# Turning the value product of a windowed attention: values as weights, probabilities moving, division ahead of the transposes

## Chip, core and metric

The kernel runs on one core of one Trainium2 chip. The metric is the device time of one launch in microseconds; the median of several runs counts. Inputs and outputs are float32.

## What is computed

Two layers of a decoder trunk over 512 positions of width 1024. In each layer three mixers work side by side on one input projection and feed one output projection; a gated feed-forward (width 2816) and a gated embedding term follow. The change touches only the third mixer, a causal attention over a window of 128 with six query heads on two key/value heads, and a learned sink per head:

```python
kb, vb = banded(k), banded(v)          # chunk c and chunk c - 1, 128 keys each
sc = einsum('bcqhgd,bckhd->bchgqk', qb, kb) * HEAD_DIM ** -0.5
sc = where(in_window & ~first_pad, sc, NEG_INF)
probs = softmax(concatenate([sc, sink], -1), -1)[..., :-1]
o = einsum('bchgqk,bckhd->bcqhgd', probs, vb)
...
mix = concatenate([y_a, y_b, y_c], -1) @ w_out[i]
```

The positions are cut into four chunks of 128 (c = 0 to 3). Chunk 0 has no chunk before it.

## The kernel before

All five engines run through one list of events, made by `plan_schedule`; each engine picks from it what is its own, in that order, and the engines wait for each other by semaphores alone. So the list sets the order of every queue. A weight strip is loaded by DMA into `raw`, rounded by ScalarE into `w_hi` (float32r, L880), and its remainder is subtracted by VectorE into `w_lo` (L1113); every large product is three float32r products (`mm3`, L616 to L618). That rounding is an event `conv`, put behind every strip, three strips ahead of its use.

The mixers are spread between the blocks of the input projection by `plan_mixers`. A slot u is one block: strip (u div 4) for the 128 positions m = u mod 4, 12 products of 384 columns (slots 12 to 35) or of 512 (36 to 43), and then what `plan_mixers` has put at u. The strips from slot 12 on are bk (12 to 19), bq (20 to 27), bv (28 to 35), a (36 to 43), bg (44 to 51). In slots 16 to 19 and 24 to 27 VectorE also has `rope_full` for each block (five operations, L1134 to L1146).

A chunk c of the attention starts at slot u = 13, 18, 24, 29 and takes these steps:

- `swa_cur` (u) and `swa_prev` (u + 1): scores of the two halves of the window (L758), each into two PSUM banks, `swa_bank(c, 0)` and `swa_bank(c, 1)` (banks 4 and 5 for even chunks, 6 and 7 for odd ones), three heads in each. ScalarE copies the first half to `prob` (L971). VectorE then overlays the second half by a predicated copy (`later_m`, L1237), so that both halves of the window lie in one tile of 128 x 128 for each head: each query sees exactly 128 keys. VectorE forms the maxima (L1239 to L1242), ScalarE the exponentials and their sums (L979) and that of the sink (L982).
- `swa_PT` (u + 4): TensorE transposes the six tiles (L766); VectorE masks them twice, lower triangle to `ptl` (L1249) and, from chunk 1 on, upper triangle to `ptu` (L1251).
- `swa_o` (u + 6): for each head one product with `ptl` and one with `ptu` as the weights (128 keys x 128 queries), 64 columns of values moving (L775, L778). The output has queries on the partitions. VectorE multiplies it by the reciprocal of the sum into `swa_y` (L1257 to L1260).
- `swa_yT` (u + 9): three transposes (L786) bring it to features on the partitions; ScalarE and VectorE split it into `y_hi` (L869) and `y_lo` (L1162).

A float32 product is two instructions in the trace, a transpose and a float32r product are one. The first retention events follow at slots 34 to 38: `ret_T` (L800), `ret_sc` (L808), `ret_o` (L821 to L830), in banks 4 and 5; `ret_T` of chunk 1 in slot 38 waits for the state that VectorE updates from `ret_o` of chunk 0 in slot 37 (L1295, L1296). `ret_T` of chunk 0 waits for y_lo of attention chunk 2, and scores of chunk c for y_lo of chunk c - 2.

Of the kernel before, what the change touches and what calls it, by code (L numbers as in the profile page):

```python
# [16 lines left out]
F32 = mybir.dt.float32  # L17
# [3 lines left out]
ALU = mybir.AluOpType  # L21
# [55 lines left out]
def plan_mixers():  # L77

    at = {}

    def put(u, *e):
        at.setdefault(u, []).append(e)

    for c in range(TILES):

        put(9 + c, "swa_T", c)
        u = (13, 18, 24, 29)[c]
        for step, name in ((0, "swa_cur"), (1, "swa_prev"), (4, "swa_PT"), (6, "swa_o"), (9, "swa_yT")):
# [193 lines left out]
TABLE_W = _at  # L282


def build_trunk(nc, depth, x_in, p_t, pre_mix, w_in, ln_w, ln_b, ws_t, bs_t, gn_w, sinks, w_out,
                post_mix, pre_ffn, w_ffn_in, w_ffn_out, post_ffn, w_gate, w_ple, ple_norm,
                table, later, out):
# [3 lines left out]
    def place(name, shape, dt, kb):  # L291
        return nc.alloc_sbuf_tensor_at(name, shape, dt, offset=BASE + int(kb * KB))
# [31 lines left out]
    swa_y = [place(f"swa_y{i}", [P, C_HEADS, HD], F32, (110, 48)[i]) for i in range(2)]  # L324
# [67 lines left out]
    def sem(name):  # L392
        sems[name] = nc.alloc_semaphore(name)
        return sems[name]
# [39 lines left out]
    swa_exp = sem("swa_exp")  # L434
    swa_PT = sem("swa_PT")
    swa_PTm = sem("swa_PTm")
    swa_o = sem("swa_o")
    swa_yr = sem("swa_yr")


    ret_T = sem("ret_T")
# [35 lines left out]
    last_use = {layer * NS + SIDX[strip]: i for (layer, strip, _), i in order_mm.items()}  # L477
    order_yT = []
    for layer, e in schedule:
        if e[0] in ("swa_yT", "ret_yT", "gmlp_yT"):  # L480
            order_yT += [(layer, e)] * (2 if e[0] == "gmlp_yT" else 1)

    def y_count(layer, e):
# [72 lines left out]
    with nc.Block() as block:  # L556
# [57 lines left out]
        def _(pe):  # L614
# [48 lines left out]
            def block_of(layer, strip, m):  # L663
                g = layer * NS + SIDX[strip]
                kind, _, i = strip
                pe.wait_ge(lo_ready, 2 * (g + 1))
                if kind == "in":
                    last = mm_in(layer, g, strip, m)
                elif kind == "out":
                    if i == 3:  # L670
                        if m < 2:
                            pe.wait_ge(*evac(layer, GNAMES[-1], 2 * m + 1))
                        if m == 2:
                            pe.wait_ge(y_lo_ready, y_count(layer, ("ret_yT", 3)))

                    need = {2: ("ret_yT", m), 3: ("swa_yT", m), 1: ("ret_yT", m), 0: ("gmlp_yT",)}[i]
                    if m == 3:
                        need = ("gmlp_yT",)
                    pe.wait_ge(y_lo_ready, y_count(layer, need))
                    last = mm_rows(y_hi, y_lo, 2 * i, g, m, i == 3, i == 0)  # L680
                elif kind == "ffn":
                    if m is not None:

                        pe.wait_ge(h_lo_ready, t_count(layer, "ffn", max(2 * m + 1, i)))
                    else:
                        if i >= 4:
                            pe.wait_ge(mid_lo_ready, layer * FCH + i - 3)
                        else:
                            pe.wait_ge(h_lo_ready, t_count(layer, "ffn", 3))
                    last = mm_ffn(layer, g, strip, m)  # L690
                elif kind == "fo":
                    if i == 0:
                        last_in_pair = max(j for j in range(FCH) if j % 4 == m)
                        pe.wait_ge(mid_lo_ready, layer * FCH + last_in_pair + 1)
                    pe.wait_ge(mid_lo_ready, layer * FCH + 2 * i + 2)
                    last = mm_rows(mid_hi, mid_lo, 2 * i, g, m, i == 0, i == FCH // 2 - 1)
                elif kind == "ple":
                    pe.wait_ge(h_lo_ready, t_count(layer, "gate", m))
                    pe.wait_ge(p_lo_ready, layer + 1)
                    last = mm_rows(p_hi, p_lo, 0, g, m, True, True)  # L700
# [25 lines left out]
            for layer, e in schedule:  # L726
# [17 lines left out]
                elif kind in ("swa_cur", "swa_prev"):  # L744
# [4 lines left out]
                    if kind == "swa_cur":  # L749
                        pe.wait_ge(swa_cT, layer * TILES + TILES)  # L750
                        if c >= 2:

                            pe.wait_ge(y_lo_ready, y_count(layer, ("swa_yT", c - 2)))
# [7 lines left out]
                    last.then_inc(swa_cur if kind == "swa_cur" else swa_prev, 1)  # L761
                elif kind == "swa_PT":
                    c = e[1]
                    pe.wait_ge(swa_exp, layer * TILES + c + 1)
                    for hh in range(C_HEADS):
                        last = pe.transpose(swa_bank(c, hh // 3)[:, (hh % 3) * P:(hh % 3 + 1) * P],  # L766
                                            prob[c % 2][:, hh, :], T_("ident"))
# [1 line left out]
                elif kind == "swa_o":  # L769
                    c = e[1]  # L770
                    pe.wait_ge(swa_PTm, layer * TILES + c + 1)
                    for hh in range(C_HEADS):
                        o = swa_bank(c, 0)[:, hh * HD:(hh + 1) * HD]
                        g = hh // 3
                        last = pe.matmul(o, ptl[c % 2][:, hh, :], cv[:, c, rows(g)], start=True, stop=(c == 0),  # L775
                                         skip_group_check=True)
                        if c:
                            last = pe.matmul(o, ptu[c % 2][:, hh, :], cv[:, c - 1, rows(g)], start=False,  # L778
                                             stop=True, skip_group_check=True)
                    last.then_inc(swa_o, 1)  # L780
                elif kind == "swa_yT":
                    c = e[1]
                    pe.wait_ge(swa_yr, layer * TILES + c + 1)
                    flat = swa_y[c % 2][:, :, :].rearrange("p h d -> p (h d)")
                    for k in range(3):
                        last = pe.transpose(swa_bank(c, 1)[:, k * P:(k + 1) * P], flat[:, k * P:(k + 1) * P],  # L786
                                            T_("ident"))
                    last.then_inc(y_T, 1)
                elif kind == "ret_T":
                    c = e[1]  # L790
                    pe.wait_ge(b_roped, layer * 2 * TILES + TILES + c + 1)
                    if c:
                        pe.wait_ge(ret_oread, layer * TILES + c)
                        pe.wait_ge(ret_state, layer * 3 + c)
                    else:

                        pe.wait_ge(y_lo_ready, y_count(layer, ("swa_yT", 2)))
# [36 lines left out]
                elif kind == "ret_yT":  # L834
                    c = e[1]
                    pe.wait_ge(ret_yr, layer * TILES + c + 1)
                    if c == 0:
                        pe.wait_ge(y_lo_ready, y_count(layer, ("swa_yT", 3)))
# [26 lines left out]
        def _(act):  # L865
# [50 lines left out]
            for layer, e in schedule:  # L916
# [48 lines left out]
                elif kind == "swa_cur":  # L965
                    c = e[1]
                    act.wait_ge(swa_cur, layer * TILES + c + 1)
                    if c >= 2:
                        act.wait_ge(y_T, y_count(layer, ("swa_yT", c - 2)))
# [5 lines left out]
                elif kind == "swa_prev":  # L975
# [113 lines left out]
        def _(dve):  # L1089
# [87 lines left out]
            for layer, e in schedule:  # L1177
# [65 lines left out]
                elif kind == "swa_PT":  # L1243
# [6 lines left out]
                        if c:  # L1250
                            last = dve.tensor_tensor(ptu[c % 2][:, h3, :], b3, mask3(T_("upT")), ALU.mult)  # L1251
                    done(last, swa_PTm)
                elif kind == "swa_o":
                    c = e[1]
                    o = c % 2
                    dve.wait_ge(swa_exp, layer * TILES + c + 1)
                    step(dve.tensor_tensor(rl[o], lsum[o], esink[o], ALU.add))  # L1257
                    step(dve.reciprocal(rl[o], rl[o]))
                    dve.wait_ge(swa_o, layer * TILES + c + 1)
                    done(dve.tensor_tensor(swa_y[o][:], heads(swa_bank(c, 0)[:, 0:BW], 6),  # L1260
                                           rl[o][:, :, None].to_broadcast([P, 6, HD]), ALU.mult), swa_yr)
                elif kind == "swa_yT":
                    c = e[1]
                    y_split(layer, e, swa_bank(c, 1)[:, 0:BW].rearrange("p (k t) -> p k t", k=3),
                            y_hi[:, 5:8, c * P:(c + 1) * P], y_lo[:, 5:8, c * P:(c + 1) * P])
                elif kind == "ret_sc":
                    c = e[1]
# [135 lines left out]
```

## Time and profile before

| | |
|---|---|
| median of 3 runs | 1348.83 us (1348.6 to 1353.02) |
| span of the profiled execution | 1344.1 us |
| TensorE products busy | 96% of the span, 6712 instructions |
| VectorE, ScalarE, GpSimd busy | 47%, 31%, 5% |
| granted TensorE clock | 1.00 except for two stretches of 3.4 and 6.8 us and the end |
| DMA | 123.5 MB, mean 92 GB/s |

The span is that of one profiled execution, 4.7 us under the median. The profile lists the busy time of each engine, groups of instructions by source line, waits with what ended them, and the chain of work that ended last. Busy time of TensorE is modelled: overlapping products make it look fuller than it is, so lengths are better read from one start to the next.

### The profile page before, as it was taken

The page shows a single profiled execution, that of the slowest core. Times are in us where ns is not written, and L with a number is a line of the kernel's source. Part 1 is how long each engine was busy: PE and PEld are TensorE (multiplying, and loading weights), DVE is VectorE, ACT ScalarE, POOL GpSimd, SP SyncE. Part 2 cuts the span into 40 slices and gives each one's busy share as a digit, 9 for nine tenths or more (in the row PEclk, how much of TensorE's full clock was granted, in tenths as well). Part 3 has the DMA queues.
Part 4 walks back from the last instruction along what each step waited for, and adds up shares of the span by engine and source line. Part 5 has one row for each costly group of instructions (what it writes and reads, how often), then busy time and mean ns, then how long its engine had stood idle before and what let it go on. Part 6 is the DMA issues. An engine that isn't in the chain of part 4 may idle for free.

```text
span 1344.1 us, 16616 instructions
## 1 busy us (share of the span) xinstructions
PE 1289.3 (96%) x6712; PEld 1112.6 (83%) x6712; DVE 634.3 (47%) x894; ACT 419.0 (31%) x722; POOL 71.6 (5%) x120
## 2 busy tenths in 40 slices
PE   6999989999999999999999998999999999999997
PEld 6988778898888888887889887879888888888876
DVE  5486574733333332227466847645433333322462
ACT  4424222432222221125343322233322222211341
POOL 1000120200000000002000002111000000000010
PEclk9999999999999999999999999999999999999999
DMA  5321124233333322342232221222433333223121
GB/s 187 114 80 53 58 63 125 65 110 95 95 101 103 105 98 95 94 141 82 64 93 71 73 65 63 95 63 64 142 95 102 103 102 101 95 94 125 63 79 63
DMA packets 123436, 123.54 MB, mean 92 GB/s; under 512 B 4576, under 2 KB 107872, under 8 KB 123360
## 3 DMA queue, kind: packets, MB, share of 16 engines
q1 hardware_dynamic: 123360, 122.49, 29.7%
q8 instruction: 53, 0.87, 0.3%
q14 instruction: 23, 0.19, 0.0%
HBM read 120.37 MB, written 2.10 MB: 91 GB/s over the span
## 4 chain that ended last, share of the span: by engine, by line
PE 69%; DVE 8%; ACT 2%; issue 1%; POOL 1%; DMA 0%; DVEq 0%; ACTq 0%; POOLq 0%
PE bank L616 22%; PE bank L618 22%; PE bank L617 22%; DVE w_lo L1113 1%; PE bank L718 1%; DVE upd L1195 1%; DVE x L1202 1%; POOL tiny L1060 1%; POOL tiny L1062 1%; ACT w_hi L880 0%; PE bank L825 0%; DVE h_lo L1175 0%; ACT junk L934 0%; ACT junk L932 0%; PE bank L775 0%
## 5 line engine op out<-in xcount | busy, mean ns | idle before, releaser
L1113 DVE TENSOR_TENSOR w_lo<-raw,w_hi 128x1024 fp32r<-128x1024 f32 (+1 forms) x220 | 258.8, 1176 | 496.0 <-ACT w_hi L880 491.0
L880 ACT ACTIVATE w_hi<-raw 128x1024 fp32r<-128x1024 f32 (+1 forms) x220 | 213.9, 1014 | 482.5 <-PE bank L618 463.7
L616 PE MATMUL bank<-h_hi,w_hi 128*128 128x512 f32 (+1 forms) x800 | 291.6, 365 | 2.6 <-DVE h_lo L1175 2.6
L617 PE MATMUL bank<-h_lo,w_hi 128*128 128x512 f32 (+1 forms) x800 | 291.1, 364 | 0.0
L618 PE MATMUL bank<-h_hi,w_lo 128*128 128x512 f32 (+1 forms) x800 | 291.1, 364 | 0.0
L616 PE MATMUL bank<-w_hi,h_hi 128*128 128x384 f32 (+2 forms) x576 | 209.0, 363 | 5.8 <-DVE h_lo L1175 4.0
L618 PE MATMUL bank<-w_hi,h_lo 128*128 128x384 f32 (+2 forms) x576 | 202.7, 352 | 0.0
L617 PE MATMUL bank<-w_lo,h_hi 128*128 128x384 f32 (+2 forms) x576 | 202.4, 351 | 0.0
L616 PEld LDWEIGHTS bank<-h_hi,w_hi 128*128 128x128 f32 x800 | 151.0, 189 | 26.9 <-issue 3.4
L618 PEld LDWEIGHTS bank<-h_hi,w_lo 128*128 128x128 f32 x800 | 151.0, 189 | 23.8
L617 PEld LDWEIGHTS bank<-h_lo,w_hi 128*128 128x128 f32 x800 | 151.0, 189 | 23.5
L616 PE MATMUL bank<-w_hi,mid_hi 128*128 128x512 f32 x352 | 137.4, 390 | 0.0
L618 PE MATMUL bank<-w_hi,mid_lo 128*128 128x512 f32 x352 | 137.1, 389 | 0.0
L617 PE MATMUL bank<-w_lo,mid_hi 128*128 128x512 f32 x352 | 137.1, 389 | 0.0
L616 PEld LDWEIGHTS bank<-w_hi,h_hi 128*128 128x128 f32 x576 | 110.5, 192 | 16.8 <-issue 7.2
L618 PEld LDWEIGHTS bank<-w_hi,h_lo 128*128 128x128 f32 x576 | 110.4, 192 | 7.7
L617 PEld LDWEIGHTS bank<-w_lo,h_hi 128*128 128x128 f32 x576 | 110.5, 192 | 7.1
L618 PEld LDWEIGHTS bank<-w_hi,mid_lo 128*128 128x128 f32 x352 | 66.1, 188 | 13.7
L617 PEld LDWEIGHTS bank<-w_lo,mid_hi 128*128 128x128 f32 x352 | 66.1, 188 | 13.7
L616 PEld LDWEIGHTS bank<-w_hi,mid_hi 128*128 128x128 f32 x352 | 66.1, 188 | 13.5
L1060 POOL TENSOR_SCALAR tiny<-tiny 128x1 f32<-128x1 f32 x24 | 12.8, 532 | 805.8 <-ACT junk L934 805.2
L957 ACT ACTIVATE mid_hi<-bank 128x512 fp32r<-128x512 f32 x44 | 26.3, 598 | 83.6 <-DVE bank L1219 83.6
(152 smaller groups left out, 1204.8 us busy)
## 6 DMA issues: line engine op xcount, KB each, us to landing
raw<-in_w_ffn_in SPq DMA_DIRECT2D x88, 512.0 KB, 4.7
raw<-in_w_ffn_out SPq DMA_DIRECT2D x44, 512.0 KB, 4.1
raw<-in_w_in SPq DMA_DIRECT2D x40, 384.0 KB, 3.7
raw<-in_w_out SPq DMA_DIRECT2D x16, 512.0 KB, 4.0
raw<-in_w_gate SPq DMA_DIRECT2D x16, 512.0 KB, 4.0
raw<-in_w_in SPq DMA_DIRECT2D x12, 512.0 KB, 4.3
x<-in_x_in SPq DMA_DIRECT2D x4, 512.0 KB, 7.9
raw<-in_w_ple SPq DMA_DIRECT2D x4, 512.0 KB, 5.3
```

Of the source, the lines that this page charges most:

```text
L616: pe.matmul(out_ap, a_hi, b_hi, start=start, stop=False, skip_group_check=True)
L617: pe.matmul(out_ap, a_hi, b_lo, start=False, stop=False, skip_group_check=True)
L618: return pe.matmul(out_ap, a_lo, b_hi, start=False, stop=stop, skip_group_check=True)
L718: last = pe.transpose(banks[2 * m + half][:, k * P:(k + 1) * P], src[:, kk * P:(kk + 1) * P], T_("ident"))
L880: act.activation(w_hi[g % SLOTS][:, j * n:(j + 1) * n], raw[q % RAWS][:, 0:n], ACT.Copy).then_inc(hi_ready, 1)
L957: act.activation(mid_hi[:, j, :], banks[2 * (j % 4) + 1][:, :], ACT.Copy).then_inc(mid_hi_ready, 1)
L1060: step(pool.tensor_scalar(t_post, ss_post[n % 2][:, 0:1], ss_post[n % 2][:, 1:2], EPS, ALU.add, ALU.add))
L1062: pool.tensor_tensor(r_post[n % 2], t_post, half_neg[:, 0:1], ALU.pow).then_inc(post_r, 1)
L1113: done(dve.tensor_tensor(w_lo[g % SLOTS][:, j * n:(j + 1) * n], raw[q % RAWS][:, 0:n], w_hi[g % SLOTS][:, j * n:(j + 1) * n].bitcast(F32), ...
L1195: last = dve.scalar_tensor_tensor(out=dst, in0=banks[2 * m + half][:, :], scalar=r_post[n % 2], in1=wrow[:, c], op0=ALU.mult, op1=ALU.mult)
L1202: done(dve.tensor_tensor(x[:, m, :], x[:, m, :], upd[:], ALU.add), x_new)
```

## The change

The probabilities are divided by their sum while queries are still on the partitions, before the transposes (new event `swa_norm` at u + 4). The value product is turned round: the values of one key/value head (128 keys x 64) are the weights, and the three heads that share them move together (384 columns). The output then has features on the partitions, 64 partitions for each key/value head, 3 x 128 queries side by side, in one bank. So the output needs no transposes, and `swa_yT` goes. As its rows now come in the order head 0, head 3, head 1, head 4, head 2, head 5, the rows of `w_out` are put into the same order on the host. The new steps are u, u + 1, u + 4 (`swa_norm`), u + 6 (`swa_PT`), u + 8 (`swa_o`, with the split into `y_hi` and `y_lo`).

```diff
@@ plan_mixers
-        for step, name in ((0, "swa_cur"), (1, "swa_prev"), (4, "swa_PT"), (6, "swa_o"), (9, "swa_yT")):
+        for step, name in ((0, "swa_cur"), (1, "swa_prev"), (4, "swa_norm"), (6, "swa_PT"), (8, "swa_o")):
@@
+def c_rows_paired():
+    first = AW + BW
+    heads = [h for j in range(3) for h in (j, 3 + j)]
+    tail = [first + h * HD + d for h in heads for d in range(HD)]
+    return np.array(list(range(first)) + tail)
@@ TensorE
                 elif kind == "swa_PT":
-                    pe.wait_ge(swa_exp, layer * TILES + c + 1)
+                    pe.wait_ge(swa_norm, layer * TILES + c + 1)
...
                 elif kind == "swa_o":
                     pe.wait_ge(swa_PTm, layer * TILES + c + 1)
-                    for hh in range(C_HEADS):
-                        o = swa_bank(c, 0)[:, hh * HD:(hh + 1) * HD]
-                        g = hh // 3
-                        last = pe.matmul(o, ptl[c % 2][:, hh, :], cv[:, c, rows(g)], start=True, stop=(c == 0),
+                    for g in range(2):
+                        last = pe.matmul(swa_bank(c, 0)[rows(g), 0:BW], cv[:, c, rows(g)],
+                                         ptl[c % 2][:, 3 * g:3 * g + 3, :], start=True, stop=(c == 0),
                                          skip_group_check=True)
-                        if c:
-                            last = pe.matmul(o, ptu[c % 2][:, hh, :], cv[:, c - 1, rows(g)], start=False,
-                                             stop=True, skip_group_check=True)
-                    last.then_inc(swa_o, 1)
-                elif kind == "swa_yT":
-                    c = e[1]
-                    pe.wait_ge(swa_yr, layer * TILES + c + 1)
...
+                    if c:
+                        for g in range(2):
+                            last = pe.matmul(swa_bank(c, 0)[rows(g), 0:BW], cv[:, c - 1, rows(g)],
+                                             ptu[c % 2][:, 3 * g:3 * g + 3, :], start=False, stop=True,
+                                             skip_group_check=True)
                     last.then_inc(y_T, 1)
@@ VectorE
-                elif kind == "swa_o":
+                elif kind == "swa_norm":
                     c = e[1]
                     o = c % 2
                     dve.wait_ge(swa_exp, layer * TILES + c + 1)
                     step(dve.tensor_tensor(rl[o], lsum[o], esink[o], ALU.add))
                     step(dve.reciprocal(rl[o], rl[o]))
-                    dve.wait_ge(swa_o, layer * TILES + c + 1)
-                    done(dve.tensor_tensor(swa_y[o][:], heads(swa_bank(c, 0)[:, 0:BW], 6),
-                                           rl[o][:, :, None].to_broadcast([P, 6, HD]), ALU.mult), swa_yr)
-                elif kind == "swa_yT":
-                    c = e[1]
-                    y_split(layer, e, swa_bank(c, 1)[:, 0:BW].rearrange("p (k t) -> p k t", k=3),
+                    done(dve.tensor_tensor(prob[o][:], prob[o][:], rl[o][:, :, None].to_broadcast([P, 6, P]),
+                                           ALU.mult), swa_norm)
+                elif kind == "swa_o":
+                    c = e[1]
+                    y_split(layer, e, swa_bank(c, 0)[:, 0:BW].rearrange("p (k t) -> p k t", k=3),
                             y_hi[:, 5:8, c * P:(c + 1) * P], y_lo[:, 5:8, c * P:(c + 1) * P])
```

ScalarE's split moves in the same way from `swa_yT` to `swa_o`, and every wait that named `swa_yT` names `swa_o`.

## Rows read from the trace of the kernel before

**Rows 1.** The page: busy time of the engines; the chain that ended last, by engine.

```profile
PE 1289.3 (96%) x6712; PEld 1112.6 (83%) x6712; DVE 634.3 (47%) x894; ACT 419.0 (31%) x722; POOL 71.6 (5%) x120
...
PE 69%; DVE 8%; ACT 2%; issue 1%; POOL 1%; DMA 0%; DVEq 0%; ACTq 0%; POOLq 0%
```

**Rows 2.** Waits, whole span: who waited for whom, us in total, times, longest.

```profile
PE bank L766 <- ACT tiny L982: 4.0, 2, 2.0
...
PE bank L775 <- DVE ptu L1251: 2.4, 4, 0.9
...
PE bank L775 <- DVE ptl L1249: 1.2, 2, 0.6
...
PE bank L758 <- DVE y_lo L1162: 1.2, 2, 0.8
```

**Rows 3.** TensorE in order of time, layer 0: start us, length us, instruction [idle before].

```profile
68.34 0.34 PE L618 MATMUL bank<-w_hi,h_lo 128*128 128x384 f32 x1
68.61 1.26 PE L758 MATMUL bank<-cT 64*128 64x128 f32 x12
...
70.08 0.34 PE L617 MATMUL bank<-w_lo,h_hi 128*128 128x384 f32 x1
...
71.84 0.34 PE L618 MATMUL bank<-w_hi,h_lo 128*128 128x384 f32 x1
72.77 1.55 PE L775 MATMUL bank<-cv,ptl 128*128 128x64 f32 x12 [0.59 <-DVE ptl L1249]
...
81.82 0.49 PE L786 MATMUL bank<-tab,swa_y 128*128 128x128 f32 x3
84.31 0.87 PE L766 MATMUL bank<-tab,prob 128*128 128x128 f32 x6 [2.00 <-ACT tiny L982]
...
89.68 0.43 PE L775 MATMUL bank<-cv,ptl 128*128 128x64 f32 x2 [0.33 <-DVE ptu L1251]
...
92.50 1.26 PE L758 MATMUL bank<-cT 64*128 64x128 f32 x12
...
112.24 0.43 PE L775 MATMUL bank<-cv,ptl 128*128 128x64 f32 x2 [0.89 <-DVE ptu L1251]
...
144.19 0.52 PE L800 MATMUL bank<-tab,bk 128*128 128x128 f32 x3 [0.91 <-DVE state L1296]
```

**Rows 4.** VectorE in order of time, layer 0, same columns.

```profile
69.06 0.56 DVE L1134 TENSOR_TENSOR rope_x<-bank,tab 128x384 f32<-128x384 f32 x1
...
71.69 1.02 DVE L1249 TENSOR_TENSOR ptl<-bank,tab 128x384 f32<-128x384 f32 x2
...
81.54 0.17 DVE L1242 TENSOR_TENSOR tiny<-tiny 128x6 f32<-128x6 f32 x1
85.09 1.95 DVE L1113 TENSOR_TENSOR w_lo<-raw,w_hi 128x768 fp32r<-128x768 f32 x2 [3.38 <-ACT w_hi L880]
87.08 0.56 DVE L1162 TENSOR_TENSOR y_lo<-bank,y_hi 128x384 fp32r<-128x384 f32 x1
...
107.72 2.48 DVE L1113 TENSOR_TENSOR w_lo<-raw,w_hi 128x1024 fp32r<-128x1024 f32 x2
110.23 0.56 DVE L1249 TENSOR_TENSOR ptl<-bank,tab 128x384 f32<-128x384 f32 x1
```

**Rows 5.** ScalarE in order of time, layer 0, same columns.

```profile
84.06 0.19 ACT L982 ACTIVATE tiny<-tiny 128x6 f32<-128x6 f32 x1
```

**Rows 6.** Groups of VectorE by form, 56 to 146 us: busy us, mean ns.

```profile
L1113 DVE TENSOR_TENSOR w_lo<-raw,w_hi 128x768 fp32r<-128x768 f32 x8 | 7.7, 959 | 7.0 <-ACT w_hi L880 6.8
...
L1239 DVE TENSOR_REDUCE tiny<-prob 128x6 f32<-128x768 f32 x4 | 3.8, 954 | 0.1
```

**Rows 7.** TensorE in order of time, retention, both layers.

```profile
173.09 0.49 PE L821 MATMUL bank<-state,kqT 128*128 128x128 f32 x2 [2.52 <-DVE scm L1270]
...
834.05 0.66 PE L821 MATMUL bank<-state,kqT 128*128 128x128 f32 x2 [2.52 <-DVE scm L1270]
```

**Rows 8.** Busy us by stretch, PE, PEld, DVE, ACT, POOL; then PEclk, DMA share, GB/s.

```profile
834.00:841.00 7.00, 6.95 (x30) 6.95 (x31) 5.76 (x14) 0.00 (x0) 1.38 (x3) 0.52 0.29 109
```

More of the change, by code:

```diff
@@ L323, in build_trunk @@
     ptu = [place(f"ptu{i}", [P, C_HEADS, P], F32, (116, 54)[i]) for i in range(2)]
-    swa_y = [place(f"swa_y{i}", [P, C_HEADS, HD], F32, (110, 48)[i]) for i in range(2)]
     cq = [place(f"cq{i}", [P, BW], F32, 113 + 1.5 * i) for i in range(2)]
@@ L436, in build_trunk @@
     swa_PTm = sem("swa_PTm")
-    swa_o = sem("swa_o")
-    swa_yr = sem("swa_yr")
+    swa_norm = sem("swa_norm")
     ret_T = sem("ret_T")
@@ L479, in build_trunk @@
     for layer, e in schedule:
-        if e[0] in ("swa_yT", "ret_yT", "gmlp_yT"):
+        if e[0] in ("swa_o", "ret_yT", "gmlp_yT"):
             order_yT += [(layer, e)] * (2 if e[0] == "gmlp_yT" else 1)
@@ L674, in block_of @@
                             pe.wait_ge(y_lo_ready, y_count(layer, ("ret_yT", 3)))
-                    need = {2: ("ret_yT", m), 3: ("swa_yT", m), 1: ("ret_yT", m), 0: ("gmlp_yT",)}[i]
+                    need = {2: ("ret_yT", m), 3: ("swa_o", m), 1: ("ret_yT", m), 0: ("gmlp_yT",)}[i]
                     if m == 3:
@@ L751, in _ @@
                         if c >= 2:
-                            pe.wait_ge(y_lo_ready, y_count(layer, ("swa_yT", c - 2)))
+                            pe.wait_ge(y_lo_ready, y_count(layer, ("swa_o", c - 2)))
                     else:
@@ L771, in _ @@
                     pe.wait_ge(swa_PTm, layer * TILES + c + 1)
-                    for hh in range(C_HEADS):
-                        o = swa_bank(c, 0)[:, hh * HD:(hh + 1) * HD]
-                        g = hh // 3
-                        last = pe.matmul(o, ptl[c % 2][:, hh, :], cv[:, c, rows(g)], start=True, stop=(c == 0),
+                    for g in range(2):
+                        last = pe.matmul(swa_bank(c, 0)[rows(g), 0:BW], cv[:, c, rows(g)],
+                                         ptl[c % 2][:, 3 * g:3 * g + 3, :], start=True, stop=(c == 0),
                                          skip_group_check=True)
-                        if c:
-                            last = pe.matmul(o, ptu[c % 2][:, hh, :], cv[:, c - 1, rows(g)], start=False,
-                                             stop=True, skip_group_check=True)
-                    last.then_inc(swa_o, 1)
-                elif kind == "swa_yT":
-                    c = e[1]
-                    pe.wait_ge(swa_yr, layer * TILES + c + 1)
[L784 to L787, printed above, removed]
+                    if c:
[3 more added lines that the diff above has]
+                                             skip_group_check=True)
                     last.then_inc(y_T, 1)
@@ L795, in _ @@
                     else:
-                        pe.wait_ge(y_lo_ready, y_count(layer, ("swa_yT", 2)))
+                        pe.wait_ge(y_lo_ready, y_count(layer, ("swa_o", 2)))
                     for i, src in enumerate((bk, bq)):
@@ L837, in _ @@
                     if c == 0:
-                        pe.wait_ge(y_lo_ready, y_count(layer, ("swa_yT", 3)))
+                        pe.wait_ge(y_lo_ready, y_count(layer, ("swa_o", 3)))
                     elif c < TILES - 1:
@@ L968, in _ @@
                     if c >= 2:
-                        act.wait_ge(y_T, y_count(layer, ("swa_yT", c - 2)))
+                        act.wait_ge(y_T, y_count(layer, ("swa_o", c - 2)))
                     for g in range(2):
@@ L1258, in _ @@
                     step(dve.reciprocal(rl[o], rl[o]))
-                    dve.wait_ge(swa_o, layer * TILES + c + 1)
-                    done(dve.tensor_tensor(swa_y[o][:], heads(swa_bank(c, 0)[:, 0:BW], 6),
-                                           rl[o][:, :, None].to_broadcast([P, 6, HD]), ALU.mult), swa_yr)
-                elif kind == "swa_yT":
+                    done(dve.tensor_tensor(prob[o][:], prob[o][:], rl[o][:, :, None].to_broadcast([P, 6, P]),
+                                           ALU.mult), swa_norm)
+                elif kind == "swa_o":
                     c = e[1]
-                    y_split(layer, e, swa_bank(c, 1)[:, 0:BW].rearrange("p (k t) -> p k t", k=3),
+                    y_split(layer, e, swa_bank(c, 0)[:, 0:BW].rearrange("p (k t) -> p k t", k=3),
                             y_hi[:, 5:8, c * P:(c + 1) * P], y_lo[:, 5:8, c * P:(c + 1) * P])
@@ L1387 @@
         "bs_t": np.asarray(gmlp_bs).transpose(0, 2, 1),
-        "gn_w": ret_gn_w, "sinks": attn_sinks, "w_out": w_out, "post_mix": norm_mix_post,
+        "gn_w": ret_gn_w, "sinks": attn_sinks, "w_out": np.asarray(w_out)[:, c_rows_paired(), :], "post_mix": norm_mix_post,
         "w_ffn_in": w_ffn_in, "w_ffn_out": w_ffn_out, "post_ffn": norm_ffn_post,
```

## The prediction

> **What bounds the kernel now.** I read the page first. TensorE is busy for 1289 of 1344 us and carries 69% of the chain that ended last; VectorE has 8% [rows 1]. So a change can win in two ways: less TensorE time, or shorter waits of TensorE. The view of waits then says which waits belong to the attention: the transposes of the probabilities (L766) wait for the last exponential, 4.0 us in two waits, the value products (L775) for the masked copies on VectorE, 2.4 and 1.2 us, the score product (L758) for a y_lo, 1.2 us [rows 2]. All come twice, once a layer. Last I read TensorE and VectorE side by side in time for layer 0, slots 13 to 38 of plan_mixers (a slot is one block of 12 products and what is put behind it). I use these durations, all taken from start to start, so that modelled ends don't enter:
>
> - A slot: ten products lie between 70.08 and 71.84, 0.176 us each, so 2.1 us for 12 [rows 3].
> - A score event (12 instructions of 64 rows): 68.34 to 70.08 is 1.74 us with two ordinary products in it, so 1.39 us [rows 3].
> - A value product event: 24 instructions from 89.68 to 92.50, 2.8 us with the step into the 64-row form, 2.65 us without; chunk 0 has 12 and costs 1.35 [rows 3]. Each instruction takes 0.11 us though only 64 elements move.
> - Three output transposes 0.33 and six probability transposes 0.65 us, at the same 0.11 each [rows 3].
>
> VectorE runs late in these slots, since each block of bk and bq costs it 2.63 us of rope (69.06 to 71.69) against a slot of 2.1. It masks chunk 0 at 71.69, while TensorE has stood since 71.84 plus one product; it splits at 87.08, and masks chunk 2 at 110.23, behind two w_lo from 107.72 [rows 4].
>
> **The change, part by part** (layer 0; layer 1 repeats it).
>
> *Value product.* Removed: 1.35 + 3 x 2.65 = 9.3 us. Added: 2 wide products for chunk 0, 4 for the others, each again two instructions (float32 is two everywhere in the trace). 384 elements move. No row shows such an instruction. Its length lies between 0.176 us (a float32r product of the same 384 elements, rows 3) and 0.33 (three times the 0.11 of a float32 one with 128 elements, rows 3). I take 0.32, since it is the same type. The second unknown is whether the two 64-column halves run beside one another. The nearest row is the 64-row form: 12 instructions in 1.26 us, of which 0.27 is the last one's length, so 11 steps in 0.99, where twelve full-array ones take 1.55 [rows 3]. Three of its steps have vanished, that is, its two halves overlap for a part. Carried over: 8 instructions in 5 steps, 1.6 us, plus what the score event costs beyond its own 0.99, 0.4 us: 2.0 us. Chunk 0: 3 steps, 0.96 + 0.4 = 1.35. Sum 7.35; gain 1.95. Bounds for four products: 1.3 us (short instructions, overlapped) and 2.8 (0.32 each, one after another, 2.56 + 0.2).
>
> The Trainium skill, TensorEngine Tiling (Array Packing), Key Properties, says that different tiles can run matmuls in parallel and that a change of the tiling mode drains the array. The trace shows both for row tiles; for column tiles no row does. By the page the price is my 2.0 or a little less. If only its drain held, it would be 2.8 or more.
>
> *Output transposes.* 4 x 0.33 = 1.3 us gone. Their PSUM to y_hi and y_lo splits stay, as part of swa_o, one slot earlier.
>
> *Division.* The 128x384 product on VectorE (0.56) becomes one of 128x768. Rows of that size take 0.96 us on VectorE, reduce and subtraction alike [rows 6]. With the two small steps swa_norm costs 1.4 us, 0.4 more than before. A broadcast factor changes nothing in the trace's mask products, so I see no bound far from this. What matters is that all of it now lies between the exponential and the transposes. Queued behind it on VectorE are ropes, w_lo and the next masks; TensorE waits for it.
>
> *New places.* Transposes 2 slots later, the products 2 later, the split 1 earlier. I follow the chain to each new wait.
>
> Slot 19: VectorE is free of its second rope at 71.69 [rows 4], divides until 73.15. TensorE arrives at 71.84 + 0.18 - 0.65 = 71.4 (the transposes are gone from slot 17), so it waits 1.8. Before: 0.6 [rows 3].
>
> Slot 21: two ropes (5.25) and the masks (1.05) end at 79.45; TensorE comes at 73.2 + 0.65 + 1.4 + 4.2 = 79.4. No wait.
>
> Slot 24: the maxima of chunk 1, before at 81.54 [rows 4], come at 82.1; the exponentials, then 84.06 + 0.19 [rows 5], at 84.6; w_lo, which ended at 87.04 [rows 4], at 87.45; split 88.05; division until 89.5 (VectorE is strictly in the order of the program, so the division stands behind w_lo and split although its input is there since 84.6). TensorE: 79.45 + 1.35 + 3 x 2.1 = 87.1. Wait 2.45. Before, slots 22 and 24 had 2.0 and 0.33 [rows 3].
>
> Slot 30: VectorE's queue up to 110.2 is the same as before (w_lo of 107.72 is its end, rows 4), then division: 111.7. TensorE: 89.55 + 0.65 + 6 slots 12.5 + three score events 4.2 + products 2.0 = 108.8. Wait 2.9. Before, slots 29 and 30 had 0.8 and 0.9 [rows 2, 3].
>
> From there VectorE is no longer late. Before, 112.24 to 144.19 is 31.95 us [rows 3]. New, from 111.7: minus 2 x 2.65 products, plus 2 x 2.0, minus 0.33, plus 0.65 (these transposes are now inside the stretch), minus 0.2 (a short wait of ret_T for the split of chunk 2, which now comes two slots ahead), minus the 0.91 wait at 144.19 [rows 3]: that wait was for the retention state, and the products of chunk 3 now stand between ret_o and it, 2.0 us of cover. 31.95 - 2.1 = 29.9, so slot 38 is reached at 141.6, 2.6 us ahead, and with the last 0.33 of transposes 2.9 to 3.1 us ahead. What comes behind (retention, gMLP) waits for chains which TensorE itself started, and shifts with it.
>
> **Sum.** 3.0 us a layer, 6.0 for both. In the terms: products 1.95 and transposes 1.3 saved, the waits grow by about 0.2. The profiled execution has 1344.1; the median 1348.83 lies 4.7 above it and goes by the same difference: 1348.8 - 6.0 = 1342.8.
>
> **Rivals.**
>
> *Halves don't overlap: the rotation saves nothing.* 28 products x 0.64 = 17.9 us against 168 x 0.11 = 18.5 removed. At slots 24 and 30 the longer products only fill a wait, but those of chunks 2 and 3 add 0.8 each: 1.4 us a layer left, 2.8 in all, 1346.0. For it: no row has a 64-column instruction. Against it: the overlap of the row halves. In this case the change doesn't do on TensorE what it is laid out for; only the transposes and the covered wait pay.
>
> The Trainium skill, FP8 and Floating Point Precision, TensorE Precision Notes, says that true FP32 takes 4 passes through the array. By it a product of 384 is 4 x 0.16 = 0.64 us, an estimate that agrees with my 2 x 0.32; the trace's 128-element rows can't tell, as 64 elements cost as much.
>
> *Short instructions.* At 0.176 each, overlapped, four products cost 1.3. Chunks 2 and 3 give 0.7 each more, of which about 0.8 is eaten by short waits at slots 34 and 38: 3.6 a layer, 7.2 in all, 1341.6.
>
> *The clock falls behind the new waits; slower.* TensorE stood 2.52 us before L821 in both layers. In layer 0 the clock stayed, in layer 1 the stretch from 834 to 841 ran at 0.52 of 2.4 GHz, that is at 1.2 [rows 7, 8]: some 6.8 us at half speed, 3.4 us of work lost. My new waits of 2.45 and 2.9 us are of that size, the old ones in these slots at most 2.0 [rows 2]. Behind slot 24 a slow stretch is hidden by the wait of slot 30; behind slot 30 nothing hides it. One in each layer costs up to 6.8 us. With the gain of 6.0 that is 1349.6, with that of the second rival 1352.8. It decides from the point where more than 6 (or 2.8) us are lost. For it: one wait in two of that length did it. Against it: one did not, and the waits in slots 22 and 24 before, 2.0 and 0.33, left it alone.
>
> **How the numbers follow.** Overlapping halves and steady clock 0.45 (1342.8, own range 1340.5 to 1344.5); no overlap 0.23 (1346.0); short instructions 0.1 (1341.6); one slow stretch with a gain left 0.15 (1344.5 to 1347); slower by the clock 0.07 (1349.6 to 1352.8). A measurement of this kernel tells about 0.5% from no change, 6.7 us: the line is at 1342.1. Below it lie the short instructions and some four tenths of the first case: 0.3 faster, 0.66 same, 0.04 slower. The range goes from 1340.0 to 1349.5.
>
> **What would show it.** Right: L775 and L778 in pairs with starts almost at one time, a score-like event of about 2.0 us; no L786; waits of L766 of 1.8, 2.4 and 2.9 us for VectorE's division in each layer and none for the exponential; no wait of L775; L800 without its wait for the state in slot 38; division of 0.96 us; granted clock 1.00 from slot 24 to 38. Wrong: starts 0.32 apart throughout (the second rival), the division clearly over 1 us, which goes straight into three waits a layer, or a clock under 1.00 behind slot 30.

## The result

| | before | changed |
|---|---|---|
| median | 1348.77 us | 1340.05 us |
| range of its runs | 1348.6 to 1353.0 | 1338.4 to 1341.2 |
| ratio, 95% interval | | 0.9931 [0.9911, 0.9952] |
| span of the profiled execution | 1344.1 | 1338.8 |
| TensorE instructions | 6712 | 6576 |
| waits for the probability transposes, both layers | 4.0 us, 2 waits | 10.7 us, 6 waits |

The change is 0.69% faster, 8.7 us. I had forecast 6.0 us, and held it likelier (0.66) that no difference could be told; the interval shows one, so that was wrong. The two profiled executions are only 5.3 us apart, and that is part of the story. The median of before is 1348.77 here and 1348.83 in the first table because one more execution was taken.

**The turned product, after.** TensorE in order of time (start us, length us, instruction), chunk 0 and then chunk 1 of layer 0. It answers to the value product rows of [rows 3].

```profile
79.51 0.34 PE L624 MATMUL bank<-w_hi,h_lo 128*128 128x384 f32 x1
79.78 0.87 PE L779 MATMUL bank<-ptl,cv 128*64 128x384 f32 x4
80.57 0.45 PE L622 MATMUL bank<-w_hi,h_hi 128*128 128x384 f32 x1
80.85 0.34 PE L623 MATMUL bank<-w_lo,h_hi 128*128 128x384 f32 x1
...
100.35 0.34 PE L624 MATMUL bank<-w_hi,h_lo 128*128 128x384 f32 x1
100.62 0.87 PE L779 MATMUL bank<-ptl,cv 128*64 128x384 f32 x4
101.31 0.81 PE L784 MATMUL bank<-ptu,cv 128*64 128x384 f32 x4
102.06 0.44 PE L622 MATMUL bank<-w_hi,h_hi 128*128 128x384 f32 x1
102.34 0.34 PE L623 MATMUL bank<-w_lo,h_hi 128*128 128x384 f32 x1
```

The form is now 128*64: 64 columns of the array. Eight instructions with 384 moving columns lie between 100.35 and 102.34, which hold two ordinary products (0.35) as well: 1.64 us for chunk 1, and 0.97 to 0.99 for chunk 0 in the same way. Eight lengths of 0.32 would be 2.56. The halves run beside one another, all the way: in the trace the two halves of a pair start 6 to 8 ns apart, and the pairs follow at 0.32 us, so there are four steps, not five.

**The new chain of waits.** The first fence is the view of waits over the whole span, the second TensorE at the three waits of layer 0, the third VectorE ahead of the second.

```profile
PE bank L772 <- DVE prob L1258: 10.7, 6, 2.9
```

```profile
73.39 0.44 PE L772 MATMUL bank<-tab,prob 128*128 128x128 f32 x2 [1.62 <-DVE prob L1258]
...
89.77 1.21 PE L772 MATMUL bank<-tab,prob 128*128 128x128 f32 x6 [2.66 <-DVE prob L1258]
...
112.82 0.87 PE L772 MATMUL bank<-tab,prob 128*128 128x128 f32 x6 [0.74 <-DVE prob L1258]
...
142.04 0.49 PE L799 MATMUL bank<-tab,bk 128*128 128x128 f32 x3
```

```profile
85.75 1.95 DVE L1112 TENSOR_TENSOR w_lo<-raw,w_hi 128x768 fp32r<-128x768 f32 x2 [3.40 <-ACT w_hi L879]
87.73 0.56 DVE L1161 TENSOR_TENSOR y_lo<-bank,y_hi 128x384 fp32r<-128x384 f32 x1
88.32 0.17 DVE L1256 TENSOR_TENSOR tiny<-tiny 128x6 f32<-128x6 f32 x1
88.53 0.19 DVE L1257 RECIPROCAL tiny<-tiny 128x6 f32<-128x6 f32 x1
88.75 0.96 DVE L1258 TENSOR_TENSOR prob<-prob,tiny 128x768 f32<-128x768 f32 x1
```

What waited for the exponential and for the masks [rows 2, 3] now waits for the division (one wait of 0.22 us for y_lo apart). The division of chunk 1 stands in VectorE's queue behind two w_lo and a split, although VectorE had stood idle for 3.40 us just ahead of them. L799 (L800 before) has lost its wait for the retention state, and starts at 142.04 against 144.19 [rows 3].

**The clock.** Busy us by stretch, PE, PEld, DVE, ACT, POOL; then the granted clock, DMA share, GB/s.

```profile
89.00:98.00 9.00, 8.23 (x40) 7.32 (x41) 7.55 (x14) 1.72 (x3) 0.00 (x0) 0.62 0.63 192
98.00:105.00 7.00, 7.00 (x42) 5.68 (x40) 6.48 (x15) 2.36 (x13) 0.00 (x0) 1.00 0.00 1
730.00:736.00 6.00, 5.27 (x28) 4.88 (x29) 5.48 (x12) 0.00 (x0) 0.00 (x0) 0.72 0.00 0
769.00:777.00 8.00, 7.67 (x33) 7.12 (x34) 4.74 (x11) 0.81 (x5) 0.00 (x0) 0.57 0.25 82
```

TensorE fell to 1.2 GHz behind three of the six new waits. The profile of before had it for 3.4 and 6.8 us [rows 8], the changed kernel's for 23.8 us in five stretches, up to 900 us; it is faster all the same.

### The profile page after: what moved, and what is told of

Same layout as the page of the kernel before. It is cut to its first block, busy times and chain, and to the rows that moved or that the text cites. A ratio compares the mean times of both kernels' runs of the same rounds, so it can differ in the third digit from the quotient of the medians.

```text
span 1338.8 us, 16336 instructions
## 1 busy us (share of the span) xinstructions
PE 1284.5 (96%) x6576; PEld 1099.6 (82%) x6576; DVE 637.4 (48%) x894; ACT 418.9 (31%) x722; POOL 71.2 (5%) x120
## 4 chain that ended last, share of the span: by engine, by line
PE 68%; DVE 8%; ACT 2%; issue 1%; POOL 1%; DMA 0%; DVEq 0%; ACTq 0%; POOLq 0%
PE bank L622 22%; PE bank L624 22%; PE bank L623 22%; DVE w_lo L1112 1%; PE bank L724 1%; DVE upd L1194 1%; DVE x L1201 1%; ACT w_hi L879 1%; POOL tiny L1061 1%; POOL tiny L1059 0%; DMA raw<-in_w_in 0%; ACT prob L978 0%; DVE h_lo L1174 0%; ACT junk L933 0%; ACT junk L931 0%
## 5 line engine op out<-in xcount | busy, mean ns | idle before, releaser
L624 PEld LDWEIGHTS bank<-h_hi,w_lo 128*128 128x128 f32 x800 | 151.0, 189 | 23.8
```

Source lines behind the costliest of these rows:

```text
L624: return pe.matmul(out_ap, a_lo, b_hi, start=False, stop=stop, skip_group_check=True)
```

## The experiments

Theory 1 at the start: the gain is TensorE work (products and output transposes), the new places only keep the longer chain from costing it, and VectorE's queue decides what they can. Its rival: the places bring the gain, and the direction of the product doesn't matter.

**The change again.**

> The changed kernel once more, beside the others of this group. Both theories: 0.993 of the kernel before, within 0.002. It also shows whether the granted clock falls at the same places again. If the slow stretches belong to the waits themselves, the waits of about 2.8 us ahead of the probability transposes of chunk 1 and chunk 2 bring them again; if they hang on chance, at least one of the four is at full clock now.

0.9933 [0.992, 0.9945]. Its half-clock stretches: 3.4 us at 91, 6.8 at 169, 3.4 at 691, 6.8 at 749, 3.4 at 831. Three of the five lie where the first profile had one (90, 172, 831). Behind the transposes of chunk 2 in layer 1 the clock stayed up this time, but TensorE had waited only 0.55 us there, not 2.94: the stretch at 749 had made it late. The waits that did reach 2.6 us (89.24 and 748.70) were both followed by a fall, as in the first profile; behind the same wait of 1.62 us for chunk 0 in layer 1 the clock fell in one profile and not in the other.

Taken over all twelve profiles of this study, between 40 and 1320 us: TensorE waited 33 times for 2.2 us or more, and in 32 of them the clock fell during the wait or within 2.1 us behind it; of 31 waits between 1.5 and 2.1 us, 10 had a fall, of 100 between 0.85 and 1.5 us, two. So the long waits bring the slow stretch nearly always, the short ones by chance.

**No overlap of the halves.**

```diff
-                        last = pe.matmul(swa_bank(c, 0)[rows(g), 0:BW], cv[:, c, rows(g)],
+                        last = pe.matmul(swa_bank(c, g)[:, 0:BW], cv[:, c, :],
                                          ptl[c % 2][:, 3 * g:3 * g + 3, :], start=True, stop=(c == 0),
...
-                            last = pe.matmul(swa_bank(c, 0)[rows(g), 0:BW], cv[:, c - 1, rows(g)],
+                            last = pe.matmul(swa_bank(c, g)[:, 0:BW], cv[:, c - 1, :],
```

> The value product with both heads' values as 128 columns of weights and an output of 128 partitions in a bank of its own for each group: the same number of instructions, the same 384 columns, but no column halves that could run beside one another. The output rows of heads 3 to 5 are then not the right ones (the split reads one bank only); the work around is the same. Theory 1 (the gain is TensorE work, and the overlap of the halves carries it): an event goes from 1.64 to 2.6 us, chunk 0 from 0.97 to 1.3; at chunks 0 and 1 the next wait swallows it, at chunks 2 and 3 it counts: 1.9 us a layer, 3.8 us in all, about 0.9960 of before. Theory 2 (the gain is the new places in the order, the products themselves don't matter): 0.993 as with the change.

0.9959 [0.9945, 0.9973]. TensorE in order of time, chunk 1 of layer 0:

```profile
99.56 0.33 PE L624 MATMUL bank<-w_hi,h_lo 128*128 128x384 f32 x1
99.73 1.45 PE L779 MATMUL bank<-ptl,cv 128*128 128x384 f32 x4
101.02 1.45 PE L784 MATMUL bank<-ptu,cv 128*128 128x384 f32 x4
102.02 0.63 PE L622 MATMUL bank<-w_hi,h_hi 128*128 128x384 f32 x1
102.49 0.34 PE L623 MATMUL bank<-w_lo,h_hi 128*128 128x384 f32 x1
```

Four instructions are 1.29 us here, 0.32 each; the event is 2.93 - 0.35 = 2.58 us against 1.64. Chunk 0 goes from 0.97 to 1.43 in the same way. Of these 6.6 us of added work in both layers only some 3.5 (0.0026 of the time) reach the end: the rest lies where TensorE waits for VectorE next. This is theory 1's number (by the medians it is 4.4 us, and both kernels had falls of the clock). It also settles both unknown sizes of the forecast: 0.32 for an instruction, and full overlap. And it shows what the turn buys on TensorE: without the overlap a turned event takes 2.58 us, where the old one took 2.65 [rows 3].

**No division.**

```diff
-                    step(dve.reciprocal(rl[o], rl[o]))
-                    done(dve.tensor_tensor(prob[o][:], prob[o][:], rl[o][:, :, None].to_broadcast([P, 6, P]),
-                                           ALU.mult), swa_norm)
+                    done(dve.reciprocal(rl[o], rl[o]), swa_norm)
```

> The changed kernel without the 128x768 division on VectorE (the probabilities go on undivided, so that part of the computation is left out). Theory 1 (VectorE's queue sets when TensorE goes on in slots 19 to 30, so each division counts whole although TensorE seems the busy engine): three divisions of 0.96 us ahead of slot 30 in each layer, so 2 us a layer earlier after what other waits take back, 4 to 5 us in all, 0.9895 to 0.9905 of before. Theory 2 (the division is beside other work, it costs what VectorE's busy time grows by, 0.4 us each, or nothing): within 1.5 us of the change, 0.992 to 0.993.

0.9914 [0.9901, 0.9928], 2.6 us below the change measured beside it. That lies between the two expectations, and neither number is met. Over six divisions it is 0.43 us each, so the time alone would fit the 0.4 us of theory 2 as well; the traces have to separate them. The first fence is the view of waits, layer 0 from 56 to 146 us, the second VectorE at the place of chunk 1's division, the third TensorE at chunk 2 of layer 1, the fourth the clock by stretch, as above:

```profile
PE bank L772 <- DVE tiny L1257: 4.2, 3, 2.0
PE bank L764 <- DVE y_lo L1161: 1.0, 1, 1.0
```

```profile
90.30 0.96 DVE L1112 TENSOR_TENSOR w_lo<-raw,w_hi 128x768 fp32r<-128x768 f32 x1 [1.21 <-ACT w_hi L879]
```

```profile
767.80 0.88 PE L772 MATMUL bank<-tab,prob 128*128 128x128 f32 x6 [1.97 <-DVE tiny L1257]
```

```profile
110.50:117.50 7.00, 7.00 (x29) 6.44 (x30) 4.47 (x10) 0.70 (x4) 0.00 (x0) 0.51 0.35 119
```

The waits at chunks 0 and 1 are each 1.0 us shorter (0.62 and 1.64 against 1.62 and 2.66). In layer 1 the transposes of chunk 2 start 76.08 us behind the layer's wait for h_lo, which ends at 691.72; in the change it is 78.01 (691.32 to 769.33): 1.9 us saved a layer, theory 1's 2 us. Of the three divisions' 2.9 us one has gone into a longer wait of VectorE for w_hi (1.21 us against 0.22). So VectorE's queue is the bound. Why these 3.9 us became 2.6 is not shown. The clock has a hand in it: in layer 0 it was at half for 6.8 us behind the transposes of chunk 2, where nothing hides it, and slot 38 came at 142.37, no earlier than in the change; in layer 1 it was the change that had the longer stretch there (6.8 us against 3.4). All this rests on one profile of each kernel.

**Old places.**

```diff
-(4, "swa_norm"), (6, "swa_PT"), (8, "swa_o")
+(4, "swa_norm"), (4, "swa_PT"), (6, "swa_o")
```

> The changed kernel with the division and the transposes at step 4 and the product at step 6, that is, the new arithmetic in the places the kernel before had. Theory 1 (places matter because exponential, division and masks now lie in one chain, and slots are the only cover they have): TensorE waits some 7 us at slot 17, 4 at 22, 7 at 28 and 4 at 33, against 1.8, 2.8 and 1 now, 12 us a layer more than the change has, 20 to 25 us in all: 1.008 to 1.012 of before. Theory 2 (the gain is TensorE work alone, places are for tidiness): 0.993 to 0.996.

1.0244 [1.0228, 1.026]: slower by 33 us than before, 41 slower than the change. First the waits in layer 0, then two stretches:

```profile
PE bank L772 <- DVE prob L1258: 22.9, 4, 7.4
```

```profile
68.00:78.00 10.00, 5.85 (x23) 5.41 (x25) 5.13 (x12) 0.00 (x0) 0.00 (x0) 0.52 0.05 17
...
116.00:127.00 11.00, 6.55 (x31) 6.16 (x32) 6.14 (x11) 0.10 (x1) 0.00 (x0) 0.57 0.29 83
```

The waits are as reckoned (22 us). The number was missed first by a wrong difference: 22 us against the change's 5.6 is 16 a layer, 33 in both, not 12 and 20 to 25. Measured, the transposes wait 45.6 us in both layers against 10.7, 34.9 more. The remaining 7 of the 41.7 us are most likely the clock, which the expectation had left out: in layer 0 it fell 2.0 and 2.4 us into the waits of over 7 us and stayed at 1.2 GHz for 10.2 us each, in layer 1, with waits of 7.2 and 7.0 us, for 6.8. The turned product in the old places loses far more than it saves.

**The kernel before, a second profile.**

> The kernel before, unchanged, for a second profiled execution. Over 16 executions it took 1345.1 to 1353.1 us, the shortest at a mean granted clock of 0.996, the longest at 0.986. Theory 1 (the execution profiled at first, 0.994, had fewer slow stretches of TensorE than most, so the sum started 2 to 3 us too low): this profile shows more stretches at half clock than the two inside the first one, and a span of 1345 to 1351 with them. Theory 2 (the spread is something else, such as transfers): a longer span with the same two stretches.

1.0001 [0.999, 1.0011] by time; this execution took 1352.2 us, span 1350.5. The first fence is TensorE in order of time, the second the clock by stretch.

```profile
112.10 0.43 PE L775 MATMUL bank<-cv,ptl 128*128 128x64 f32 x2 [0.90 <-DVE ptu L1251]
```

```profile
114.00:121.00 7.00, 7.00 (x31) 6.66 (x31) 3.08 (x7) 0.37 (x2) 0.00 (x0) 0.51 0.00 0
780.00:787.00 7.00, 7.00 (x28) 6.78 (x29) 3.08 (x7) 2.06 (x11) 0.00 (x0) 0.53 0.00 0
```

Same waits in the attention, same DMA as in the first profile, but five half-clock stretches between 100 and 900 us instead of two. The two in the fence follow a wait of 0.9 us and value products of 64 columns. Slot by slot against the first profile, 2.9 us are lost at 114, 1.6 at 698 and 2.8 at 780, and the stretches in the retention change little, since waits follow them. Over 16 executions the time roughly follows the mean granted clock: 1345.1 us at 0.996, 1347.2 to 1350.5 at 0.991, 1353 at 0.986. Theory 1 holds.

**The changed kernel and the kernel before, waits filled.**

```diff
+            def fill(bank, n):
+                for _ in range(n):
+                    pe.transpose(bank[:, 0:P], T_("ident"), T_("ident"))
...
+                    pe.wait_ge(swa_m, layer * TILES + c + 1)
+                    fill(swa_bank(c, 0), (12, 20, 12, 0)[c])
                     pe.wait_ge(swa_norm, layer * TILES + c + 1)
```

In the kernel before (0, 16, 0, 0) ahead of the wait for `swa_exp`; in both also `fill(banks[6], 20)` ahead of the waits of `ret_o` of chunk 2 and `ret_T` of chunk 3.

> The changed kernel, with idle transposes of the identity ahead of the waits of TensorE: 12, 20 and 12 (1.3, 2.1, 1.3 us) ahead of the waits for the divisions of chunks 0, 1, 2, and 20 each ahead of the longest waits of the retention (slots 45 and 46), into banks that are free there. They only fill the waits. Theory 1 (the clock falls because TensorE stands still, and the fall costs time where no later wait hides it): no stretch below full clock between 60 and 1330 us, mean clock above 0.993, and 2 to 4 us less than the change: 0.990 to 0.992 of before, with a smaller spread. Theory 2 (slow stretches come of themselves or are hidden by waits anyway): 0.993 or, by the fillers that stick out, 0.994 to 0.995.

0.9916 [0.9903, 0.993], 1337.5 us, clock 0.997 to 0.998, range 0.8 us. One half-clock stretch of 3.4 us was left inside.

> The kernel before, with idle transposes of the identity ahead of its three waits of over 2 us in each layer: 16 ahead of the wait for the exponentials of chunk 1, 20 each ahead of slots 45 and 46. Theory 1 (the spread of the kernel before, 1345 to 1353, is slow clock behind its waits): the clock stays up, the spread shrinks, and the median falls to 1343 to 1345.5, 0.995 to 0.998. The change's gain against this one, at steady clock for both, is then what its work and places are worth. Theory 2: 1.000, spread as before.

0.9979 [0.9968, 0.9991], 1346.1 us, range 1343.3 to 1348.7: faster, but short of the 1343 to 1345.5 expected. The waits of 0.9 and 0.6 us were not filled, and the clock still varied from 0.995 to 0.999; the executions at 0.998 or more took 1343.3 to 1346.0. So idle time filled with work that nobody needs makes both kernels faster, and the clock is what it keeps up (for the change the two intervals overlap, but no execution of one reaches the times of the other: 1337.1 to 1337.9 against 1338.2 to 1340.1). Both filled, the change is 8.6 us ahead by the medians; against those executions of the kernel before with a steady clock it is some 7 us ahead (1344.4 their mean, 1337.5).

**Division put into the idle time of VectorE.**

```diff
-        for step, name in ((0, "swa_cur"), (1, "swa_prev"), (4, "swa_norm"), (6, "swa_PT"), (8, "swa_o")):
+        n, t, o = ((1, 3, 7), (1, 5, 7), (2, 6, 7), (1, 5, 8))[c]
+        for step, name in ((0, "swa_cur"), (1, "swa_prev"), (n, "swa_norm"), (t, "swa_PT"), (o, "swa_o")):
```

> The changed kernel with other places only: division at steps 1, 1, 2, 1 for chunks 0 to 3 (for chunks 0, 1 and 3 right behind the maxima, ahead of the next w_lo and ropes in VectorE's queue), transposes at 3, 5, 6, 5, products at 7, 7, 7, 8. Theory 1 (VectorE's queue is the bound of slots 16 to 30 and stood idle while ScalarE formed exponentials; a division put there costs nothing): the waits of L772 go from 1.8, 2.8 and 1 us in each layer to about 1.3, 1.3 and 0, TensorE is 3 to 4.5 us earlier at slot 38 of each layer, 6 to 9 us in all: 0.986 to 0.989 of before. Theory 2 (the wait only moves on, to the masks and the splits): 0.991 to 0.994, with new waits of L779 or L764 of 2 us and more.

0.9861 [0.9847, 0.9875], 1330.0 us: faster than both kernels. VectorE in order of time around the division of chunk 1, then TensorE's waits in layer 0, then TensorE at slot 38:

```profile
80.86 0.17 DVE L1242 TENSOR_TENSOR tiny<-tiny 128x6 f32<-128x6 f32 x1
83.69 0.17 DVE L1257 TENSOR_TENSOR tiny<-tiny 128x6 f32<-128x6 f32 x1 [2.66 <-ACT tiny L982]
83.89 0.19 DVE L1258 RECIPROCAL tiny<-tiny 128x6 f32<-128x6 f32 x1
84.12 0.96 DVE L1259 TENSOR_TENSOR prob<-prob,tiny 128x768 f32<-128x768 f32 x1
85.11 0.96 DVE L1113 TENSOR_TENSOR w_lo<-raw,w_hi 128x768 fp32r<-128x768 f32 x1
```

```profile
PE bank L773 <- DVE prob L1259: 2.3, 2, 1.3
PE bank L780 <- DVE ptu L1251: 1.4, 1, 1.4
```

```profile
136.32 0.49 PE L800 MATMUL bank<-tab,bk 128*128 128x128 f32 x3
```

The division is done at 85.1, where it was done at 89.7, and w_lo starts at 85.11 instead of 85.75. It takes place while ScalarE forms w_hi (from 83.49). It isn't wholly free: between the last exponential and w_lo there were 0.84 us in the change (84.91 to 85.75) and are 1.53 now (83.58 to 85.11), so half of the 1.4 us lies in time that was idle. Slot 38 comes at 136.3: 5.7 us ahead of the change's first profile, 4.5 ahead of its second (140.8), 7.9 ahead of the kernel before. Transposes and products moved together with the division, and no run moved the division alone.

**The same arithmetic as before, better places.**

```diff
-        for step, name in ((0, "swa_cur"), (1, "swa_prev"), (4, "swa_PT"), (6, "swa_o"), (9, "swa_yT")):
+        t, o, y = ((3, 5, 7), (5, 7, 8), (5, 7, 8), (3, 8, 9))[c]
+        for step, name in ((0, "swa_cur"), (1, "swa_prev"), (t, "swa_PT"), (o, "swa_o"), (y, "swa_yT")):
```

> The kernel before, its arithmetic untouched, with other places only: transposes of the probabilities at steps 3, 5, 5, 3 of chunks 0 to 3, value products at 5, 7, 7, 8, output transposes at 7, 8, 8, 9. By the same reckoning that gave the places of e5 TensorE's waits in slots 13 to 38 shrink from 6.7 to 2.1 us a layer. Theory 1 (half of what e5 gained over the kernel before is to be had without turning the product; VectorE's queue is the bound in both): 4.5 us a layer less, 9 in all, 0.992 to 0.995 of before, and e5 stays 6 to 9 us faster than this. Theory 2 (only the turned product makes these places possible): 0.998 to 1.002.

0.9906 [0.9891, 0.9922], with the waits of layer 0 down to these:

```profile
PE bank L776 <- DVE ptl L1250: 1.4, 1, 1.4
PE bank L787 <- DVE swa_y L1261: 0.3, 1, 0.3
```

That is a little better than expected: 1336.9 us, faster than the change itself. The kernel before had a median of 1350.8 us in this group and 1348.3 in the one of the early division, which makes the ratio look better by up to 0.2%. With places reckoned for each, turning the product is worth 0.9906 against 0.9861, 0.45% or 6 us (6.9 by the medians), and their intervals don't meet. So neither theory of the start was whole. Places alone bring 11 to 14 us, about twice what the turn brings on top of them; and the two don't simply add, since in the old places the turn loses 33 us.

**Early division, retention waits filled.**

> The kernel of e5 with 20 idle transposes of the identity each ahead of the waits of slots 45 and 46 in the retention, the only waits of over 2 us that it still has between its start and its end. In e5's profile a stretch of 6.8 us at half clock stood behind one of them in each layer. If these stretches cost time, 1 to 2 us less than e5, 0.985 of before, clock 0.997 or more; if the wait of slot 46 hides them, the same time as e5 within 0.7 us.

0.9837 [0.9824, 0.9851], 1328.4 us, clock 0.998 to 0.999, the fastest kernel of this study. Against the kernel with the early division it is 1.7 us by the medians; the 3.2 by the ratios contain the slower kernel before of this group, and the intervals overlap by a little. The profile has no half-clock stretch between 40 and 1320 us, where that of the early division had two of 6.8.

## Why the forecast was wrong where it was

**The base: the step that failed.** The sum was 6.0 us, set off from the median with the words that it "goes by the same difference". It doesn't. The profiled execution of before was one with a high clock (0.994), near the fast end; the median carries some 3 us more, and the second profile shows half-clock work of that kind in places where the kernel before hides nothing: behind slot 30's product and at the start of layer 1. By the filled versions half-clock stretches cost the change 2.0 us, and the kernel before some 4 (1348.3 against 1344.4, the mean of the six executions with a steady clock). The gain splits accordingly: 6.9 us of work and waits at a steady clock, and 1.9 us because the change loses less to the clock. The forecast of 6.0 had the first term 0.9 too small, and the second at nothing, or as a loss. Either this term or the product's, below, would by itself have put the sum past the line of 6.7 us.

From the profiled execution itself the sum would have given 1344.1 + 1.7 (what lies around the span, 1340.52 against 1338.8 in the changed kernel's profiled execution) - 6.0 = 1339.8, against 1340.05 measured. That this is so close is partly luck: the product was priced 1.4 us too high, and the changed kernel ran at a clock of 0.990 where the base had 0.994.

**Value product: mechanism right, size off.** 0.32 us an instruction was right. "8 instructions in 5 steps" was wrong, taken from the score event whose groups of six overlap only in part. Two alternating column halves overlap wholly: 4 steps, 1.64 us for an event against my 2.0, and 0.99 against 1.35, 1.45 us a layer. Half of it, that of chunks 2 and 3, lies where no wait swallows it: 1.4 us in all. The rival of no overlap is refuted for this kernel, and the run without overlap shows what it would have been: 0.9959, where I had reckoned 1346.0 or 0.998.

**Output transposes and the short wait of slot 38: right.** The trace after has no transposes of the output, and L799 waits for nothing at 142.04. The 0.2 us that I took off for a wait of ret_T of chunk 0 stayed, though: L799 waits 0.22 us for y_lo at 125.29.

**Division: right in size and place.** 0.96 us, and 1.4 with the small steps. The waits of layer 0 were forecast at 1.8, 2.45 and 2.9 us: measured 1.62, 2.66 and 0.74. The third is short because TensorE came late: 6.8 us at half clock behind slot 24, of which the wait of slot 30 hid the larger part, as the third rival had said, but not all. That stretch also held back VectorE's next steps, so the division of chunk 2 ended at 112.8, not 111.7. Slot 38 was reached at 142.04, where I had 141.6.

**The clock as a rival: seen, and on the wrong side.** I priced it as a loss of the change alone. It fell behind the new waits in three of six cases, as feared. But the kernel before had such losses too, and in most of its executions more than in the one I read. My count of "one wait in two" was also short: in that same trace TensorE waited 2.85 us until 181.00 in the retention, and the clock was at half for 3.4 us from 182.3. The wait of 2.52 us in layer 0 that I held against the rival is the only one of the 33 long waits that no fall followed.

**What I did not ask.** I took the order of events as given, and so did not see from [rows 4] that VectorE stands idle for 3.38 us ahead of w_lo at 85.09, with the exponentials of chunk 1 done at 84.25 [rows 5]. Only the last 0.84 us of it lie behind these exponentials. A part of the change's price lay there; with transposes and products moved too, the new places brought 9 us more.

## What to carry to other kernels

When an operation moves from behind a product to in front of it, look in the queue of its engine for the idle time just ahead of it: put in order before the next long job, not behind it, the same division cost less, and the places (11 to 14 us alone) were worth about twice the turned product (6 to 7 us). Time both arithmetics at places fitted to each before giving either the credit. And before a difference of half a per cent is forecast, compare the granted clock of the profiled execution with that of the other runs: a sum made on one execution should be set off from that execution's own time, and what each kernel loses to the clock is a term of its own.

## What the runs showed of the chip

- Products with 64 columns of weights, for the two halves of the output partitions in turn, run beside one another also in float32: 8 instructions of 384 columns in 1.64 us, against 2.58 for the same with 128 columns of weights. The Trainium skill, TensorEngine Tiling (Array Packing), Key Properties, says that different tiles can run matmuls in parallel. The trace agrees, for column halves too.
- A float32 instruction with 128 columns of weights takes 0.11 us with 64 or with 128 moving elements [rows 3], and 0.32 with 384. So 24 instructions with 64 moving elements (2.65 us) cost as much as 8 with 384 (2.58) when nothing overlaps.
- In the twelve profiles TensorE's clock fell to 1.2 GHz at 32 of 33 waits of 2.2 us or more, at 10 of 31 between 1.5 and 2.1 us, and at two of 100 between 0.85 and 1.5; it stayed there for 3.4 or 6.8 us, and for 10.2 twice, in waits of over 7 us. Filling waits with idle transposes brought 2 us in the changed kernel.
